# A two-layer trunk step: router and last projection tiles written in another order, router tables built between the first experts

## The reference, cut to what matters

```python
x = x + g1 * (mixer(h) @ w_o)                 # mixers of both layers: attention and a gated MLP
h = rms_norm(x, g_norm2) * (1 + sc2) + sh2
lg = h @ w_rg + b_rg                          # 4 group logits
gmask = one_hot(argmax(lg)); pg_sel = softmax(lg)[argmax]
le = (h @ w_re + b_re).reshape(-1, 4, 8)      # 32 expert logits, 8 of the picked group count
wk, ik = top_k(softmax(le of that group), 2); wk = wk / sum(wk)
hh = silu(h @ w1[e]) * (h @ w3[e]) * gate     # 32 experts of 1024 x 256, only two per token have a gate
x = x + g2 * sum_e(hh @ w2[e])
```

## Time and profile before

| what | us |
|---|---|
| median of 3 runs | 1179.8 (1178.7 to 1184.48) |
| the profiled execution | 1184.69 |
| its span, first to last instruction | 1182.8 |
| PE busy | 935.0 (79%) |
| DVE busy | 371.8 (31%) |
| ACT busy | 230.9 (20%) |
| POOL busy | 139.4 (12%) |

### The profile page before, as it was taken

How to read it: one execution, slowest core, us unless ns; L and a number is a source line. 1 busy time by engine, 2 the same in 40 slices (tenths; PEclk the granted TensorE clock), 3 DMA queues, 4 the chain that set the end, 5 groups by cost and what they waited for, 6 DMA issues and landing times.

```text
span 1182.8 us, 14805 instructions
## 1 busy us (share of the span) xinstructions
PE 935.0 (79%) x5469; PEld 552.8 (47%) x5469; DVE 371.8 (31%) x934; ACT 230.9 (20%) x585; POOL 139.4 (12%) x161
## 2 busy tenths in 40 slices
PE   4999698874998888788078988999659988888860
PEld 1445255354654554445045554554545545454540
DVE  1121562336211111111143564663362111111104
ACT  2110232101111111111033444441101111111110
POOL 0000400000122121211200000001001212111102
PEclk9999797975999999999679998998669999999995
DMA  9978999160699999996610018106808999999834
GB/s 385 401 300 349 405 422 416 77 214 0 247 415 415 417 416 417 415 390 257 245 50 26 1 71 320 46 11 250 325 9 337 418 416 416 416 416 414 330 131 160
DMA packets 70892, 330.22 MB, mean 279 GB/s; under 512 B 12440, under 2 KB 13464, under 8 KB 47416
## 3 DMA queue, kind: packets, MB, share of 16 engines
q1 hardware_dynamic: 51136, 282.55, 59.2%
q0 software_dynamic: 17840, 42.52, 9.7%
q10 hardware_dynamic: 1872, 4.56, 1.1%
HBM read 315.32 MB, written 34.62 MB: 296 GB/s over the span
## 4 chain that ended last, share of the span: by engine, by line
PE 52%; DMA 29%; DVE 9%; issue 5%; ACT 2%; SPq 2%; POOL 0%; DVEq 0%; ACTq 0%
DMA ring<-in_l_w 24%; PE psum L638 9%; PE psum L796 6%; PE psum L652 4%; PE psum L589 4%; DMA ring<-in_l_w_ada 3%; PE psum L853 3%; PE psum L485 3%; PE psum L1004 2%; PE psum L893 2%; PE psum L902 2%; PE psum L738 2%; SPq L374 2%; PE psum L621 2%; PE psum L934 1%
## 5 line engine op out<-in xcount | busy, mean ns | idle before, releaser
L638 PE MATMUL psum<-ring,scratch 128*64 128x256 f32 x2112 | 249.2, 389 | 67.2 <-DMA ring<-in_l_w 63.9
L638 PEld LDWEIGHTS psum<-ring,scratch 128*64 128x64 f32 x2112 | 168.0, 140 | 132.3 <-issue 79.2
L1715 DVE TENSOR_TENSOR scratch<-scratch,psum 64x256 f32<-64x256 f32 x64 | 27.2, 424 | 404.1 <-ACT scratch L1139 404.1
L652 PE MATMUL psum<-ring,scratch 128*64 128x512 f32 x528 | 127.7, 604 | 1.7 <-ACT scratch L1143 0.9
L2119 POOL DMA_INDIRECT expert_rows<-scratch,slot_rows x64 | 63.3, 989 | 393.3 <-ACT scratch L1153 377.6
L1139 ACT ACTIVATE scratch<-psum 64x256 f32<-64x256 f32 x64 | 24.1, 376 | 327.1 <-PE psum L638 323.9
L796 PE MATMUL psum<-ring,scratch 128*128 128x512 f32 x192 | 72.6, 539 | 1.3 <-DVE scratch L1802 1.3
L1153 ACT COPY scratch<-psum 128x512 f32<-128x512 f32 x64 | 37.5, 586 | 146.2 <-PE psum L652 146.2
L485 PE MATMUL psum<-ring,scT 128*32 128x512 f32 x320 | 43.2, 664 | 15.7 <-DMA ring<-in_l_w_ada 15.1
L652 PEld LDWEIGHTS psum<-ring,scratch 128*64 128x64 f32 x528 | 33.1, 136 | 46.1 <-issue 42.5
L796 PEld LDWEIGHTS psum<-ring,scratch 128*128 128x128 f32 x192 | 36.4, 190 | 36.6 <-issue 35.5
(11 more groups left out here) (294 smaller groups left out, 1120.9 us busy)
## 6 DMA issues: line engine op xcount, KB each, us to landing
ring<-in_l_w SPq DMA_DIRECT2D x198, 1024.0 KB
ring<-in_l_w_ada SPq DMA_DIRECT2D x48, 1024.0 KB, 4.9
expert_rows<-constants POOLq DMA_DIRECT2D x21, 512.0 KB, 40.5
ring<-in_l_w_o SPq DMA_DIRECT2D x8, 1024.0 KB
ring<-in_l_w_in SPq DMA_DIRECT2D x4, 1024.0 KB
gate_rows<-gate_rows_hbm POOLq DMA_DIRECT2D x8, 512.0 KB, 8.3
scale_shift<-gate_rows_hbm POOLq DMA_DIRECT2D x8, 512.0 KB, 11.7
ring<-in_l_w_in SPq DMA_DIRECT2D x4, 768.0 KB
```

Source lines behind the costliest of these rows:

```text
L638: last = nc.tensor.matmul(ps[64 * n:64 * n + 64, 2 + par, 0:DE], mine[:, k, :], ring[:, (slot + n) % RING, k * DE:(k + 1) * DE], start=k = ...
L652: last = nc.tensor.matmul(ps[64 * n:64 * n + 64, 5 + par, :], hhT[:, par, k, :], ring[:, slot, k * D + n * 512:k * D + (n + 1) * 512], sta ...
```

## The change

**Order on TensorE.** In layer 0 tiles 0 and 1 of the mixer's result are both transposed ahead of the first projection, into separate PSUM banks, tile 2 between the first and the second; h of tile 0 is transposed between the second and the third projection, h of tile 1 behind the third. In layer 1 h of tile 0 is transposed between the two sample projections, h of tile 1 behind them. PSUM banks change with it (`h_bank`, `LOGITS_BANK`). VectorE and ScalarE get their copies at the matching places.

```diff
+        H_BANK = ((2, 0, 4), (2, 6, 4))
+        LOGITS_BANK = (6, 0)
+        def h_bank(stage, t):
+            return H_BANK[stage // 2][t] if stage % 2 else 2 * t
...
+            def transpose_cat(n):
+                pe.wait_ge(S["att_ready"], 4 * (n + 1))
+                if n == 2:
+                    pe.wait_ge(S["catT_act"], 1)
+                    pe.wait_ge(S["catT_dve"], 1)
+                for k in range(KD):
+                    last = nc.tensor.transpose(ps[:, 2 * (n % 2) + k // 4, k % 4 * P:(k % 4 + 1) * P],
+                                               cat0[:, n, k * P:(k + 1) * P], ident)
+                last.then_inc(S["catT_in_psum"], 1)
+            def out_projection(n):
+                base = 4 + 2 * (n % 2)
+                pe.wait_ge(S["catT_act"], n + 1)
+                pe.wait_ge(S["catT_dve"], n + 1)
                 if n == 1:
                     pe.wait_ge(S["m_ready"], 5)
+                if n == 2:
+                    pe.wait_ge(S["x_updated"], 1)
                 for k in range(KD):
...
-                transpose_h(2 * l + 1, hp, 0)
-                transpose_h(2 * l + 1, hp, 1)
...
-                for t in range(NT):
-                    for s in range(t + 1):
-                        nc.tensor.matmul(ps[:, 7, t * NE:(t + 1) * NE], tri if s == t else ones[:, :],
-                                         picks[:, s, :], start=s == 0, stop=s == t)
+                nc.tensor.matmul(ps[:, 7, 0:4 * NE], con[:, C_TRI:C_TRI + P], picks, start=True, stop=False)
                 for s in range(NT):
-                    last = nc.tensor.matmul(ps[:, 7, NT * NE:(NT + 1) * NE], ones[:, :], picks[:, s, :],
-                                            start=s == 0, stop=s == NT - 1)
+                    last = nc.tensor.matmul(ps[:, 7, (s + 1) * NE:4 * NE], ones[:, :], picks[:, 0:(NT - s) * NE],
+                                            start=False, stop=s == NT - 1)
                 last.then_inc(S["rank_in_psum"], 1)
-                pe.wait_ge(S["nover_ready"], l + 1)
-                nc.tensor.matmul(ps[:, 6, 0:NE], view(W, RB + 300, P)[0:NE, :], con[0:NE, C_TRI:C_TRI + NE],
-                                 start=True, stop=True).then_inc(S["ofs_in_psum"], 1)
...
-            for t in range(NT):
-                out_projection(0, t, t, cat0[:, t, :], t == 2)
+            transpose_cat(0)
+            transpose_cat(1)
+            out_projection(0)
+            transpose_cat(2)
+            out_projection(1)
+            transpose_h(1, hp, 0)
+            out_projection(2)
+            transpose_h(1, hp, 1)
...
-            for t in (1, 2):
-                project_sample(t)
+            project_sample(1)
+            transpose_h(3, hp, 0)
+            project_sample(2)
+            transpose_h(3, hp, 1)
...
             def rms(stage, tiles=range(NT)):
+                if stage:
+                    nc.scalar.activation(warm[:, :], eps[:, :], ACT.Sqrt)
                 for t in tiles:
...
+                               ps[:, 2 * (n % 2), :].rearrange("p (k q) -> p k q", k=4)).then_inc(S["catT_act"], 1)
...
             evac_cat(0)
             evac_cat(1)
+            evac_cat(2)
             rms(1, (0,))
-            evac_cat(2)
+            evac_h(1, h2T, 0)
             rms(1, (1,))
-            evac_h(1, h2T, 0)
+            evac_h(1, h2T, 1)
             rms(1, (2,))
-            evac_h(1, h2T, 1)
             evac_h(1, h2T, 2)
...
                 dve.wait_ge(S["logits_in_psum"], 3 * (l + 1))
...
+                first_max(lgg, con[:, C_PRI4:C_PRI4 + NG], key4, top[0], gmask, NG)
                 V.tensor_tensor(gexp, lgg, over(top[0], 2, [P, NT, NG]), ALU.subtract).then_inc(S["gexp_in"], 1)
+                link(V.tensor_scalar(key4, gmask, -NEG, NEG, ALU.mult, ALU.add))
...
+                first_max(le, pri, key, top[1], pick2[0], NE)
+                link(V.scalar_tensor_tensor(out=le, in0=pick2[0], scalar=NEG, in1=le, op0=ALU.mult, op1=ALU.add))
+                first_max(le, pri, key, top[2], pick2[1], NE)
+                V.tensor_tensor(picks_by_tile, pick2[0], pick2[1], ALU.add).then_inc(S["picks_ready"], 1)
...
                 dve.wait_ge(S["rank_in_psum"], l + 1)
+                ranks = ps[:, 7, 0:NT * NE].rearrange("p (t n) -> p t n", t=NT)
+                link(V.scalar_tensor_tensor(out=slotm[:, :, 0:NE], in0=ranks, scalar=1.0, in1=picks_by_tile,
+                                            op0=ALU.add, op1=ALU.mult))
+                one_hot(0, 0)
+                V.tensor_copy(rank, ranks)
                 link(V.tensor_copy(cnt, ps[:, 7, NT * NE:(NT + 1) * NE]))
...
+                one_hot(1, 1)
+            def route_blocks(l):
+                if l == 0:
+                    modulation_columns(1, 5)
+                V.tensor_scalar(nover, cnt, float(SLOTS), None, ALU.is_gt)
+                link(V.tensor_scalar(jumps, rank, float(SLOTS), None, ALU.is_ge))
+                link(V.tensor_copy(blk, jumps))
+                for n in range(2, MAX_BLOCKS):
+                    V.scalar_tensor_tensor(out=nover, in0=cnt, scalar=float(SLOTS * n), in1=nover,
+                                           op0=ALU.is_gt, op1=ALU.add)
...
+                V.scalar_tensor_tensor(out=mod, in0=jumps, scalar=-float(SLOTS), in1=rank, op0=ALU.mult, op1=ALU.add)
+                link(V.tensor_copy(scan[0][:, 16:], nover))
+                for n in range(5):
+                    src = scan[n % 2]
+                    link(V.tensor_tensor(scan[(n + 1) % 2][:, 16:], src[:, 16:], src[:, 16 - 2 ** n:16 + NE - 2 ** n], ALU.add))
+                link(V.tensor_tensor(ofs, scan[1][:, 16:], nover, ALU.subtract))
+            def route_tokens(l):
+                link(V.scalar_tensor_tensor(out=first_row, in0=ofs, scalar=-1.0, in1=pri, op0=ALU.add, op1=ALU.add))
...
+                for k in range(2):
+                    V.tensor_tensor(key, pick2[k], blk, ALU.mult)
+                    link(V.tensor_tensor(le, pick2[k], mod, ALU.mult))
+                    V.tensor_reduce(blks[:, k, :], key, AX, ALU.add)
+                    link(V.tensor_reduce(mods[:, k, :], le, AX, ALU.add))
...
+            def route_overflow(l):
+                for k in range(2):
...
                 V.tensor_copy(ovi[0:1, l, 15:16], n1[:, NE - 1:NE]).then_inc(S["route_ready"], 1)
+            def route_gates(l):
+                dve.wait_ge(S["gexp_out"], l + 1)
+                link(V.tensor_reduce(pg, gexp, AX, ALU.add))
+                dve.wait_ge(S["eexp_out"], l + 1)
+                V.reciprocal(pg, pg)
+                link(V.tensor_scalar(wk[:, :, 0], e21, 1.0, None, ALU.add))
+                link(V.reciprocal(wk[:, :, 0], wk[:, :, 0]))
+                link(V.tensor_tensor(wk[:, :, 1], e21, wk[:, :, 0], ALU.mult))
+                link(V.tensor_tensor(gates[:, :, :], wk, over(pg, 2, [P, NT, 2]), ALU.mult))
...
-                with dve.Fori(0, LOOPED) as i:
+                route_blocks(l)
+                product(0, 0)
+                ahead(0, 0, 0)
+                route_tokens(l)
+                product(1, 1)
+                ahead(1, 0, 1)
+                route_overflow(l)
+                product(2, 2)
+                ahead(2, 1, 2)
+                route_gates(l)
+                product(3, 3)
+                ahead(3, 1, 3)
+                with dve.Fori(1, LOOPED) as i:
                     for u in range(4):
...
             evac_cat(0)
+            evac_cat(1)
             residual(0, 0, None)
-            evac_cat(1)
+            evac_cat(2)
             norm(1, 0)
             residual(1, 1, None)
-            evac_cat(2)
+            evac_h(1, h2T, 0)
             norm(1, 1)
+            evac_h(1, h2T, 1)
             residual(2, 2, 0)
             norm(1, 2)
-            for t in range(NT):
-                evac_h(1, h2T, t)
+            evac_h(1, h2T, 2)
             router(0)
+            experts(0)
             dve.wait_ge(S["route_ready"], 1)
-            experts(0)
...
             evac_out1(len(ATT1) - 1)
+            norm(3, 0)
             residual_sample(1)
-            norm(3, 0)
+            evac_h(3, h2T, 0)
             norm(3, 1)
+            evac_h(3, h2T, 1)
             residual_sample(2)
             norm(3, 2)
-            for t in range(NT):
-                evac_h(3, h2T, t)
+            evac_h(3, h2T, 2)
             router(1)
+            experts(1)
             dve.wait_ge(S["route_ready"], 2)
-            experts(1)
```

232 lines of the change are left out of this document (78 added, 154 removed).

## The result

The changed kernel takes 1138.5 us (median of 4 runs, 1136.0 to 1140.2) against 1181.6 for the kernel before beside it: ratio 0.9635, interval 0.9601 to 0.9669. Run twice more in the experiments it took 1144.0 (ratio 0.967, 0.9634 to 0.9706) and 1142.8 (0.9664, 0.9631 to 0.9697). So the gain is 39 to 43 us; the forecast was 37.3 of gain and 1142.5 us of time.

The account below looks back on a forecast made before the run. The DMA weight stream ends both expert stages, so time saved ahead of it counts in full. Layer 0 23.4, table 1.3 and layer 1 12.55 make 37.3 us off: 1142.5 against the median 1179.8, range 1133 to 1151.

Parts of the forecast that it names:

- The base: Time taken out ahead of the first expert's first half step starts and ends the weight stream earlier by the same amount.
- Layer 0, projections: Three projections of layer 0, with only transposes left between them: 6.0 us saved.
- Projection's end to logits: Behind the last projection, logits of tiles 0 and 1 hidden beside tile 2's norm chain: 5.9 us saved in each layer.
- The clock there: Tile 2's transposes and logits: TensorE stays at 1.2 GHz, since PE idles some 4.4 us ahead of them.
- Rival 1: TensorE still at 2.4 GHz when tile 2's h comes: 2.7 us less per layer, 1137; chance 0.25.
- Picks: Router's picks, with fewer but wider instructions: 5.6 us against 5.69 before, 0.1 saved.
- ranks: Rank products in 8 records in place of 18: 1.95 us against 4.15, 2.2 saved.
- tables: From ranks to first gather, one wide step and the one-hot: 1.0 us against 10.92, 9.9 saved.
- First piece: VectorE's first piece ahead of the first expert's product makes it late: 0.7 us lost in layer 0, 0.35 in layer 1.
- Rival 2: VectorE's pieces between the first experts are on the path: 25 us back, 1167; chance 0.14, whole or in part.
- Root table: Start of layer 1: the 1.28 us table load between squares and root runs while ScalarE waits, 1.3 us saved.
- Layer 1, projections: Layer 1's sample projections: tile 0's transposes between them wait for late gate rows, a 3.2 us stall; 5.2 us lost.

Follow-up runs that it names:

- the repeats: The changed kernel run twice more with no edit: 1144.0 and 1142.8 us.
- the five versions: Changed kernel with one edit each: layer 0 in old order 1155.4, nine rank products 1147.5, no early root 1142.4, all pieces up front 1162.1, longer pieces 1151.1 us.

## Why the prediction came out right, step by step

**The base.** Taking time out ahead of the first expert moved the end of the stream by as much: the shift is 27.5 us at the first expert and 28.8 at the end of layer 0's stage. First to last `up` went from 260.4 to 259.0 and from 259.0 to 260.2. The text allowed 1 us and called the base wrong if the stages were longer by more; layer 1's is longer by 1.2. That bound was too tight: with nothing edited in them the stages vary by 1.9 and 2.8 us over the profiles, and both changes lie inside that. The first `up` of layer 1 is 45.5 us earlier and the last 44.3, so the base holds to about 1 us and is not shown closer.

**Layer 0, projections** (forecast 6.0, measured 9.0): the one term of layer 0 that was mis-sized. The gaps went as told. But the step "the start is 1.1 later" failed: the sixteen transposes took 2.85 us in place of the 3.8 of the forecast (twice 1.91), because the clock rose to 2.4 GHz among them, they began 0.27 earlier, and the first projection started at 196.5 as before. Stretches from there:

```profile
194.00:196.00 2.00, 2.00 (x12) 2.00 (x11) 0.95 (x3) 0.58 (x1) 0.70 (x1) 0.55 1.00 420
196.00:198.00 2.00, 2.00 (x9) 1.12 (x8) 0.80 (x2) 0.59 (x2) 2.00 (x4) 1.00 1.02 428
```

And all three ran at 13.73, so the 15.49 and 15.67 of the earlier trace rows went to 13.73 both (3.7 us), of which 0.7 and 1.7 had been counted. The old order, put back, gave 51.3 again and slow projections behind both gaps, so what the clock takes behind the gaps belongs to the order. Whether the first one's slow start (1.8 us) was the old order's or that execution's stays open: with the old order put back the clock was up there.

**Projection's end to logits** (5.9, measured 6.1 and 6.1) was right, with the late start of tile 2's chain in it: forecast 1.85, it was 1.5 (239.47 ends the projection, 241.06 starts the residual, against 0.08 before), and with tile 1's transposes inside the projection the tail lost 1.5.

**The clock there** stayed at 1.2 GHz for tile 2, as forecast, but not for the reason given. The forecast had it fall 4 us into 4.4 us of idling, as in the earlier trace rows. It fell at 243.6, while TensorE still worked on the logits of tiles 0 and 1 (until 243.96), and in all 12 profiles with the new order in layer 0 (in three of them tile 1's transposes stand inside the projection) within 0.5 us of those logits' end. So the margin of 0.4 us on which Rival 1 was weighed did not decide anything, and that the outcome was right is luck at this step. Why it falls so early after the new order no run shows.

```profile
242.00:244.00 2.00, 1.96 (x17) 1.82 (x16) 1.50 (x2) 0.43 (x1) 0.00 (x0) 0.90 0.94 383
244.00:246.00 2.00, 0.00 (x0) 0.00 (x0) 0.82 (x2) 1.01 (x3) 0.00 (x0) 0.50 0.05 14
```

**Picks** (0.1, measured 0.2 and 0.2), **ranks** (2.2, measured 2.2; nine products gave 2.1 back) and **tables** (9.9, measured 9.9) came out as summed.

**First piece** (0.7 and 0.35 lost): the product started 0.52 us behind its Silu's end in layer 0 and 0.22 in layer 1, where 0.03 to 0.10 is the least, so it was some 0.4 and 0.1 late, and TensorE waited 0.67 and 0.36 for it. In the length of the stage it can't be seen, so "lost for good" is not shown. The later pieces were hidden, with a slack that is real but thin (0.84 and 0.92 us left ahead of the next two products); a little more work there would have been part of Rival 2. On VectorE the unlinked steps L1632 and L1633 started 0.09 us apart and linked ones 0.20 to 0.29, as the forecast had read from the earlier trace rows. The Trainium skill (VectorE: DVE Perf Modes, Terms) has a flush behind every instruction before the next can issue; on these sizes the trace again shows no such price for an instruction on whose result nobody waits.

**Root table** (1.3, measured 1.3; taking the early root away gave 1.3 back). The Trainium skill (ScalarE: Activation LUTs, What ACT_TABLE_LOAD costs) would have made it 2.7 with its drain; the squares' end, the load and the root follow each other with 0.02 us between, so no drain is on this path.

**Layer 1, projections** (5.2 lost, measured 7.0, and 4.7 and 6.3 in the repeats; up to 7.9 in the versions that leave it as it is): the mechanism was the one named, a gap ended by VectorE's norm because of late rows. The stall forecast at 3.2 was 3.16, 3.45 and 5.11; it is long when the first projection is fast (14.0 in place of 15.1 forecast), since the rows are tied to their issue and not to TensorE: projection and stall add up to 19.0 to 19.1 us in all three, where the forecast had 18.3. (Over the five versions with this place unedited it is 18.5 to 20.4, with rows that land 12.1 to 13.9 us behind the last issue; two of the stalls, 6.3 and 6.4, are beyond the forecast's bound of 5.) Of the 1.8 us that were missing, 0.8 is that, 0.9 is that the transposes ran at 1.2 GHz, and 0.1 is the second projection, whose loss of 0.9 to the clock had been put in. Together with the 6.1 behind, this part gains nothing in layer 1 (forecast 0.7), which the old order there confirmed.

**What was not forecast**: layer 1's attention was 4.5 us shorter in the profiled execution. In the repeats it was 1.6 and 4.4 shorter, and 201.5 to 205.3 in the experiments, with no edit in it. It goes with the granted clock, as said at the repeats (0.94 before, 0.95 in the changed kernel's first profile), so it is more likely spread that happened to help than a gain of the change. It is a part of why the profiled executions are 44.4 us apart where the sum said 37.3: 2.8 from layer 0's projections, 4.5 here, 2.1 in the first expert stage, less 1.8 in the sample projections and 1.5 behind layer 1's gather, make 6.1 of the 7.1; the rest is 0.3 and less in each other stage. The total was thus closer than its terms, as misses of both signs stood in it.

## What to carry to other kernels

When one stream bounds a stage, look at what stands between its last stop and its restart: here 10 us of tables on one engine stood at full length ahead of the restart, and as 13 us of pieces behind it they made one product 0.4 us late. Put the shortest piece at the first place, since only what exceeds the other engine's time counts there. And before a consumer is moved forward, look at when its operand is issued and landed: the same transposes that stalled TensorE for 3 to 6 us between two projections cost only their own 0.87 us per tile some 7 us later.

## What the runs showed of the hardware that was not expected

- Behind gaps of 3.2, 3.5 and 5.1 us at the same place of the same kernel the clock stayed up, fell 1 us behind the gap's end, and fell within the gap: the three second projections took 13.73, 15.43 and 15.05 us. The price of such a gap isn't fixed. In the five versions with this place unedited it fell behind the gap once (3.3 us) and within it four times (5.0 to 6.4 us).
- TensorE's clock can fall while the engine is at work: in 242 to 244, with TensorE busy 1.96 of 2 us on products of 36 columns, the mean granted clock was 0.90, and 0.50 behind it.
- The last of four row loads of 512 KB lands 10.1 and 10.4 us behind its issue with the weights held back, and 12.1 to 13.9 beside them.
- The same first 190 us of program take up to 8.8 us more or less, and the granted clock goes with it.
